# Differential attention by pairs of heads, with its scores, weighted sums and head norm placed between and inside projection slots

## What is computed

```
def diff_attention(xn, k_sh, v_sh, w_q, lam_params, subln_g, w_out, lambda_init):
    H, d = DIFF_HEADS, DIFF_HEAD_DIM                      # 8, 64
    q = (xn @ w_q).reshape(B, S, H, 2, d) * (d ** -0.5)
    lam = jnp.exp(jnp.sum(lp[0] * lp[1])) - jnp.exp(jnp.sum(lp[2] * lp[3])) + lambda_init
...
        s = jnp.einsum('bqhcd,bkhcd->bhcqk', qb, k_sh).astype(jnp.float32)
        s = jnp.where(kpos[None, :] <= qpos[:, None], s, -jnp.inf)
        p = jax.nn.softmax(s, axis=-1)
        a = p[:, :, 0] - lam * p[:, :, 1]
        return jnp.einsum('bhqk,bkhe->bqhe', a.astype(v_sh.dtype), v_sh)
...
    o = rms_norm(o, subln_g) * (1.0 - lambda_init)
    return o.reshape(B, S, H * 2 * d) @ w_out
```

## Time and profile before

| | us |
|---|---|
| median of 3 runs | 1465.35 |
| lowest, highest | 1465.29, 1469.29 |
| the profiled execution | 1465.31 |
| its span in the trace | 1463.5 |

### The profile page before, as it was taken

The page is one execution under the profiler, slowest core; times in us unless marked ns, Lnnn a source line. Parts: engine busy times, 40 slices in busy tenths (PEclk is TensorE's granted clock), DMA queues, the critical chain, the costliest instruction groups (busy, mean ns, idle before and its releaser), DMA issues.

```text
span 1463.5 us, 25191 instructions
## 1 busy us (share of the span) xinstructions
PE 1409.9 (96%) x9905; PEld 1301.1 (89%) x9905; DVE 914.7 (62%) x1162; ACT 697.6 (48%) x976; POOL 209.6 (14%) x142
## 2 busy tenths in 40 slices
PE   8999898998999999999999999999999997999998
PEld 8999888977998989988899997899987995899986
DVE  6875652046554577754584447688755677599964
ACT  5553355441222354433534455566654555566652
POOL 0000254302322000000000032022310000024410
PEclk9999999798999999999999999999999998999999
DMA  7444333120000445555455434455564440455553
GB/s 291 175 173 144 113 119 112 58 89 27 0 1 1 154 163 194 180 185 190 170 176 182 146 123 171 171 175 194 176 216 172 173 160 29 144 180 193 175 213 115
DMA packets 30315, 213.05 MB, mean 146 GB/s; under 512 B 3488, under 2 KB 3616, under 8 KB 5152
## 3 DMA queue, kind: packets, MB, share of 16 engines
q1 hardware_dynamic: 29088, 206.72, 40.1%
q0 software_dynamic: 1152, 5.24, 1.0%
HBM read 210.90 MB, written 1.05 MB: 145 GB/s over the span
## 4 chain that ended last, share of the span: by engine, by line
PE 87%; DVE 6%; ACT 4%; issue 2%; POOL 1%; DMA 1%; DVEq 0%; ACTq 0%; POOLq 0%; SPq 0%
PE lin L514 53%; PE lin L583 19%; PE aux L1991 2%; PE aux L2003 1%; PE aux L2001 1%; PE aux L1865 1%; PE aux L2072 1%; PE lin L620 1%; ACT whi L488 1%; POOL al L703 1%; PE aux L2084 1%; DVE wlo L495 1%; PE aux L1895 1%; DVE ht L1233 1%; DVE ro L1634 1%
## 5 line engine op out<-in xcount | busy, mean ns | idle before, releaser
L495 DVE TENSOR_TENSOR wlo<-raw,whi 128x2048 fp32r<-128x2048 f32 x176 | 409.5, 2331 | 190.4 <-ACT whi L488 190.1
L514 PE MATMUL lin<-xhi,whi 128*128 128x256 f32 (+1 forms) x1776 | 507.9, 286 | 1.8 <-DVE xlo L1244 1.8
L514 PE MATMUL lin<-xlo,whi 128*128 128x256 f32 (+1 forms) x1776 | 505.1, 284 | 0.0
L514 PE MATMUL lin<-xhi,wlo 128*128 128x256 f32 (+1 forms) x1776 | 502.7, 283 | 0.0
L488 ACT CAST whi<-raw 128x2048 fp32r<-128x2048 f32 x193 | 367.0, 1904 | 221.2 <-DMA raw<-in_stream 194.8
L514 PEld LDWEIGHTS lin<-xhi,whi 128*128 128x128 f32 x1776 | 334.9, 189 | 4.8 <-issue 4.0
L514 PEld LDWEIGHTS lin<-xhi,wlo 128*128 128x128 f32 x1776 | 337.1, 190 | 0.0
L514 PEld LDWEIGHTS lin<-xlo,whi 128*128 128x128 f32 x1776 | 335.7, 189 | 0.3
L681 POOL TENSOR_TENSOR wlo<-raw,whi 128x2048 fp32r<-128x2048 f32 x17 | 79.1, 4650 | 547.7 <-ACT whi L488 547.5
L1722 DVE SCALAR_TENSOR_TENSOR ft<-fy,par,ft 128x254 f32<-128x254 f32 (+1 forms) x176 | 90.9, 557 | 5.9 <-DVE ft L1722 0.2
L583 PE MATMUL lin<-whi,flo 128*128 128x512 f32 x176 | 69.8, 397 | 0.0
(11 more groups left out here) (378 smaller groups left out, 2295.2 us busy)
## 6 DMA issues: line engine op xcount, KB each, us to landing
raw<-in_stream SPq DMA_DIRECT2D x193, 1024.0 KB, 4.9
gp<-in_gains POOLq DMA_DIRECT2D x6, 512.0 KB, 3.9
c<-in_const SPq DMA_DIRECT2D x1, 1652.0 KB, 17.2
h<-in_x SPq DMA_DIRECT2D x2, 544.0 KB, 4.2
ht<-in_xtok POOLq DMA_DIRECT2D x1, 1024.0 KB, 6.8
c<-in_const POOLq DMA_DIRECT2D x1, 1024.0 KB, 5.0
out<-ht SPq DMA_DIRECT2D x1, 512.0 KB, 2.6
out<-ht SPq DMA_DIRECT2D x2, 256.0 KB, 2.2
```

The costliest lines, as they stand in the source:

```text
L495: nc.vector.tensor_tensor(wlo[:, s0 % 4], raw[:, s0 % 4], whi[:, s0 % 4].bitcast(F32), ALU.subtract).then_inc(lo_ready, 1)
L514: ins = nc.tensor.matmul(out, a, b, start=start and n == 0, stop=stop and n == 2)
```

## The change

- Keys and queries become one stream part `dkq` of 8 slots, in the order `DIFF`: keys 0, 1, 2, queries 0, 1, 2, keys 3, queries 3.
- Scores of pair n come as soon as both its slots are there: after slots 4, 5, 7 and after value slot 0.
- The weighted sums run by pairs of heads, each pair for both t (`HEAD_STEPS`), behind value slots 1, 2, 2 and 3.
- The head norm runs in two groups of four heads: group 0 around value slot 3 (its spread inside the slot), group 1 inside output slots 0 and 1. `keep_warm` around it is gone.
- The output slots change order: slot j belongs to half j % 2 and to heads of group j // 2, so slots 0 and 1 need heads 0-3 only.
- `dsq`, `dhi`, `dlo` move to memory that keys, queries and `x2` held.
- On ACT `x2hi` stands ahead of the conversions of slots 3 and 4; on DVE `x2lo` stands ahead of the eviction of slot 2. `lam` stands between them.

```diff
+DIFF = [("dk", 0), ("dk", 1), ("dk", 2), ("dq", 0), ("dq", 1), ("dq", 2), ("dk", 3), ("dq", 3)]
+HEAD_STEPS = [(t, 2 * n + q) for n in range(4) for t in range(2) for q in range(2)]
...
-        for t in range(2):
-            for hh in range(H1):
+        for n in range(4):
+            for t, hh in HEAD_STEPS[4 * n:4 * n + 4]:
                 use(hh % 2, f"dt{t}_{hh}")
                 if hh % 4 == 3:
-                    use(2 + hh // 4, f"dp{t}_{hh // 4}")
-        use(0, "ndsum")
-        for n in range(4):
-            use((n + 1) % 4, f"nd{n}")
+                    use(2 + t, f"dp{t}_{hh // 4}")
+            if n >= 2:
+                use(0, f"ndsum{n - 2}")
+                use(1, f"nd{2 * n - 4}")
+                use(0, f"nd{2 * n - 3}")
...
+            if name == "do":
+                return j % 2, j // 2
...
+            for b in range(4):
+                after(act, f"turn_diff{b}")
+            for kt in range(KT):
+                nc.scalar.activation(x2hi[:, kt], hf[:, kt // 2, kt % 2], ACT.Copy, scale=pcol("b_pre", kt))\
+                    .then_inc(S("x2hi"), 1)
...
+            def values(j):
...
+                ins.then_inc(pair_free[u % 2], 1)
+                load_hi(s + 3, 0)
...
+            for j in range(8):
+                load_hi(FIRST["dkq"] + j + 3, 0)
+                if j == 1:
+                    act.wait_ge(S("lam"), 1)
+                    nc.scalar.activation(lamt[:, 2:4], lamt[:, 0:2], ACT.Exp).then_inc(S("lam_exp"), 1)
+                if j >= 5:
+                    exponentials(j - 5)
+            values(0)
             exponentials(3)
...
+            values(1)
+            turned(0)
+            values(2)
+            turned(1)
+            heads_out(0)
+            turned(2)
+            heads_root(0)
+            values(3)
+            heads_high(0)
+            turned(3)
+            heads_out(1)
+            heads_root(1)
+            heads_high(1)
...
+            for k in range(2):
+                project(k)
...
+            for kt in range(KT):
+                dve.wait_ge(S("x2hi"), kt + 1)
+                ins = nc.vector.scalar_tensor_tensor(x2lo[:, kt], hf[:, kt // 2, kt % 2], pcol("b_pre", kt),
+                                                     x2hi[:, kt].bitcast(F32), ALU.mult, ALU.subtract)
+            ins.then_inc(S("x2lo"), 1)
+            project(2)
+            project(3)
...
+            project(4)
+            masked(0)
+            project(5)
+            masked(1)
+            project(6)
+            difference(0)
+            masked(2)
+            project(7)
+            difference(1)
+            load_lo(FIRST["dv"] + 3, 0)
+            masked(3)
+            difference(2)
+            load_lo(FIRST["dv"] + 4, 0)
+            difference(3)
+            load_lo(FIRST["dv"] + 5, 0)
+            heads_norm(0)
             load_lo(FIRST["dv"] + 6, 0)
-            dve_head_norm(dve, own, "nd", "subln")
+            heads_low(0)
+            heads_norm(1)
+            heads_low(1)
...
+            def project(k):
...
+                if k == 3:
+                    pe.wait_ge(S("x2lo"), 1)
...
+            project(0)
+            pe_spread("diff")
+            for k in range(1, 5):
+                project(k)
+            scores(0)
+            project(5)
+            scores(1)
+            project(6)
+            project(7)
+            scores(2)
+            values(0)
+            scores(3)
+            values(1)
+            weighted(0)
+            values(2)
+            weighted(1)
+            weighted(2)
+            heads_sum(0)
+            values(3, lambda: heads_spread(0))
+            weighted(3)
+            pe_post_layer(pe, "do", dhi, dlo, "ndlo", KT, lambda end: end // 2, between)
```

More of the change, by code:

```diff
@@ L586, in pe_post_layer @@
                         ins.then_inc(S("tile_" + tag), 1)
+                    if c == 0 and between:
+                        between(j)
                 ins.then_inc(slot_done, 1)
@@ L1116, in act_second @@
                 ins.then_inc(pair_free[u % 2], 1)
[L1117 to L1120, removed]
-            exponentials(3)
[L1122 to L1134, removed]
-                        g = hh // 4 - 1
-                        b = full(act, f"dp{t}_{g}")
-                        is_free(nc.scalar.copy(do[:, 4 * g:4 * g + 4, t * P:t * P + P], wide(b[:], P)), f"dp{t}_{g}")
-                        if t:
-                            act_head_squares(act, "nd", g)
-                if t == 0:
-                    load_hi(FIRST["dv"] + 6, 0)
@@ L1142, in act_second, with turned, heads_out @@
-            head_norm_act(act, "nd")
+                load_hi(s + 3, 0)
+            def turned(n):
+                for t, hh in HEAD_STEPS[4 * n:4 * n + 4]:
+                    W = P + t * P
+                    b = full(act, f"dt{t}_{hh}")
+                    k = HEAD_STEPS.index((t, hh))
+                    if k >= 2:
+                        weighted_sum_done(act, k - 2)
+                    is_free(nc.scalar.copy(aT[:, hh % 2, 0:1 + t], wide(b[:, 0:W], P)), f"dt{t}_{hh}")
+            def heads_out(g):
+                for t in range(2):
+                    b = full(act, f"dp{t}_{g}")
+                    is_free(nc.scalar.copy(do[:, 4 * g:4 * g + 4, t * P:t * P + P], wide(b[:], P)), f"dp{t}_{g}")
+                for t in range(2):
+                    after(act, f"dp{t}_{g}")
+                a = slice(4 * g, 4 * g + 4)
+                nc.scalar.activation(dsq[:, a], do[:, a], ACT.Square).then_inc(S("ndsq"), 1)
@@ new lines, in heads_root, with heads_high @@
+            def heads_root(g):
+                pair_done(act, pair_first["dkq"] + 7)
+                b = full(act, f"ndsum{g}")
+                if g:
+                    for n in (0, 1):
+                        full(act, f"nd{n}")
+                is_free(nc.scalar.activation(rhead[0:4, 0:SEQ], b[0:4, 0:SEQ], ACT.Sqrt, scale=1.0 / P,
+                                             bias=eps[0:4, 0:1]), f"ndsum{g}")
+            def heads_high(g):
+                for n in (2 * g, 2 * g + 1):
+                    after(act, f"nd{n}")
+                    a = slice(2 * n, 2 * n + 2)
+                    nc.scalar.copy(dhi[:, a], do[:, a]).then_inc(S("ndhi"), 1)
```

168 lines of the change are left out of this document (110 added, 58 removed).

## The result

| | before | after |
|---|---|---|
| median, us | 1465.32 | 1481.53 |
| lowest, highest | 1464.06, 1469.29 | 1480.06, 1484.19 |
| profiled execution | 1465.31 | 1481.37 |
| its span, mean granted clock | 1463.5, 0.974 | 1479.6, 0.968 |

The ratio is 1.0103, with a 95% interval of 1.009 to 1.0116. The prediction had the sign (slower, 0.81), but its 1474.5 stood for +9.2, and 16.2 was measured. The time lies outside the range of 1468 to 1479.

A forecast was written before the change was run, and what follows sets the result against it. PE was taken as the bound before, DVE as the bound of the stretch to the first sums. Layer +4.6, clock +3.4 and turn +1.2 made +9.2 on 1465.31, giving 1474.5 us; range 1468 to 1479.

The forecast's parts named there:

- sign (slower, 0.81): The whole kernel gets slower by more than 0.3% (4.4 us), chance 0.81.
- steps 1 to 5: Waits of PE: 3.7 us at `x2lo`, 7.3 at first sums, 5.3 at pairs 1 and 2, 7.0 last pair, none in output slots.
- 0.65 for rounding `dhi`: At the last pair, ACT rounds `dhi` before it copies, adding 0.65 us to a wait of 6.35.
- step 2: At pair 0's first product PE waits 7.3 us for `aT`, behind DVE's 37.9 us chain with queued conversions; bounds 5.5 and 9.5.
- The turn: At the passage to the next layer, DVE starts half 1 later: +1.2 us, bounds 0 and 2.3.
- The clock: Falls behind the waits of 7.3 and 6.4 us lose 1.7 us each: +3.4, bounds 0 and 5.
- nearer to 3.3 than to 4.43: `x2lo`'s 3.7 us wait was counted without clock loss: 3.3 us idle had kept full clock, 4.43 had halved it.
- rival A: `x2lo`'s wait before slot 3 drops the clock too: +2.1 us, 1476.6, chance 0.27.
- rival C: Short idle times at pairs 1 and 2 drop the clock: some 2 us more, 1476.5, chance 0.04.
- Rival B: At the long waits the clock costs nothing, as PE works little there: -3.4 us, 1471.1, chance 0.08.
- E: DVE's chain is some 3 us shorter and the last wait partly hidden: +0 to +4, 1465.3 to 1469.5, chance 0.09.
- D: Queued conversions don't delay `x2lo`, first sums and last pair: 14.0 us of waits and 3.4 of clock less, 1457.1, chance 0.10.

The follow-up runs named there:

- e1: The changed kernel with `x2lo` on DVE directly behind slot 0's eviction, ahead of the conversions of slots 3 and 4, and `lam` behind slot 1's eviction: 1476.15 us.
- e2: The changed kernel with output slot 14's conversions moved behind group 1's copies (ACT) and scaling (DVE), and group 0's rounding ahead of slot 11's eviction: 1475.78 us.
- e3: The changed kernel with value slot 10 and its eviction ahead of pair 0's sums and copies, slot 13's ACT conversion behind pair 1's copies: 1475.86 us.
- e4: The changed kernel with unused matmuls on ones in PE's three long waits (before slot 3, at pair 0, behind slot 11): 1475.97 us.
- e6: The changed kernel with only the spread of the head roots reading 128 partitions instead of 4: 1481.04 us.
- e10: e4 with the spread of the head roots reading 128 partitions instead of 4: 1473.34 us.
- e9: e7 with slot 13's conversion behind pair 2's copies on ACT and behind group 0's scaling on DVE: 1455.46 us.
- e5: The changed kernel with the edits of e1, e2 and e3 together: 1461.53 us, ratio 0.9962 to the kernel before.
- e7: e5 with the spread of the head roots reading 128 partitions instead of 4: 1456.90 us.
- e8: e7 with slot 13's conversion moved as in e9, and DVE's conversion of slot 17 moved behind the last residual: 1454.96 us.

## Why the prediction was off

**The waits (steps 1 to 5) were right.** By place, predicted and measured: slot 3 3.7 and 3.63; first products 7.3 and 6.81; pair 1 2.8 and 2.66; pair 2 1.9 and 1.76; last pair 7.0 and 6.33; output slots none and none. DVE's chain from the end of slot 4 (1164.36 less its semaphore) to the end of the fourth masking (1202.2) took 37.9 us, as walked through. What was too large was the 0.65 for rounding `dhi`: ACT's rounding from 1246.00 lies beside PE's transposes. Behind slot 3 the waits give 17.6 instead of 19.0, 1.4 less. PE's other work and short idle times take 99.3 us instead of 98.5 (97.9 and the four short waits of 0.15), 0.8 more. e1 (slot 3) and e2 (last pair) confirm their causes, since the wait went when the named conversions were taken from ahead of it, and so does e3 for pair 1. Pair 0's conversions were not moved in any run: e3 only filled the wait with a slot, and the first product came 78.7 us after the layer's start (1210.71 - 1132.02), where it had come after 77.9. That the conversions of slots 10 to 12 cost it what step 2 says was thus walked through but not tried.

**The turn** was predicted at +1.2. From the last output matmul to the next layer it took 4.60 us before and 6.03 after: +1.4.

**The clock is the step that failed.** It was entered as two falls of 1.7 us each, +3.4, "bounds 0 and 5". Measured are 10.5 us lost, 7.1 more than entered. The price itself was read low: 0.68 over the 7 us from 1211 is 4.5 us at half speed, not 4.2, and with the 0.57 us from 1210.43 on it is 5.0. With 0.2 for the start, -1.4, +0.8 and 0.2 at the turn the 7.1 come to 6.9, and 9.2 + 6.9 = 16.1, the distance of the profiled executions. That long waits drop the clock was right: with ones in the three of them, e4 kept it full there. Of the 7.1:

- The two counted falls cost 2.5 and 3.1 instead of 1.7 each: 2.2 more. The one at the last pair reached into the first output matmuls (from 1250.95 to about 1253), which are dense work.
- `x2lo`'s wait of 3.63 dropped the clock: 1.45. "nearer to 3.3 than to 4.43" was the wrong way to place it. This is rival A, given 0.27, with 2.1 as its price.
- Pairs 1 and 2: 1.7. This is rival C, given 0.04. Against it the prediction held that 2.31 us were passed at full clock. That was one case, and it went the other way in all six kernels with waits of 2.66 and 1.55 to 1.76 there. In four of the six (e1, e4, e6, e10) the clock fell 1.3 to 1.8 us after the wait of 2.66 ended, before the second idle time began, so the second isn't needed. PE's timeline and windows of e1:

```profile
1215.85 0.49 PE L2282 MATMUL aux<-aT,dv 128*128 128x128 f32 x2 [2.66 <-ACT aT L1135]
...
1220.91 0.80 PE L2282 MATMUL aux<-aT,dv 128*128 128x128 f32 x2 [1.55 <-ACT aT L1135]
```
```profile
1217.00:1219.00 2.00, 1.98 (x11) 1.94 (x10) 0.96 (x1) 0.89 (x3) 0.00 (x0) 0.56 0.14 57
```

- The fall behind the spread in slot 11: 1.7. No rival had it, though the trace of before shows one like it: the clock is 0.53 at 1238 to 1243, and at half from 1236 on, within and behind a spread over 8 partitions, with ones around it and no idle time of over 0.5 us (PE's timeline of before). The prediction read that fall as part of the old order's cost that goes away.

```profile
1233.25 4.62 PE L2084 MATMUL aux<-rstd,c 8*128 8x256 f32 x16 [0.42 <-DVE rstd L1568]
```

The mistake in method behind the two middle items is the same: a threshold was drawn through three idle times of one trace. That of 3.3 us, the lower bound, had a fall in e9 with the same work around it, so what passed once was no bound. A and C together, 1478.6 by the prediction, were each seen and each held improbable as if they depended on different facts; both follow once the threshold is in doubt. Rival C drew on the Trainium skill, "TensorE: Matmul & The Clock Gate", section "A second HAM failure mode: psum-queue depth-cycling", by which short idle times between groups of matmuls let the clock go down and up. The runs agree for pairs 1 and 2 (e3: a fall behind 1.90 us), though not each time: in e9 1.88 and 1.76 us passed at full clock.

**Rival B** fell with the 10.5 us lost, **E** with DVE's chain, which took its full 37.9 us, and the last wait of 6.33. **D** was wrong for this kernel, since the conversions do stand in the way. Its arithmetic was a fair guide to what the order could give: it had 14.0 us of waits from queued conversions, and e5, whose three moves go at the same waits, has 15.3 less. That the two are so close is partly luck, since in e5 a value slot fills most of pair 0's wait, which D did not have. This is where the expected gain of the change went.

**What stays open.** Why the same idle time or the same spread drops the clock in one kernel and not in another: 1.90 us did in e3, 1.87 to 1.89 at the same place in e5, e7, e8 and e9 did not; the 3.3 us at 360 us did in one of twelve profiles; 4 partitions in slot 11 did in five kernels and not in e1. The length of an idle time alone doesn't decide it. Whether a kernel has the same falls in each of its executions is open too, as each has one profile. Which of e6's other falls were longer by chance wasn't separated either.

## What to carry over

When independent work is moved between dense slots, walk through every queue that feeds it: here a weight conversion of 2 us, not urgent, stood ahead of an instruction that PE waited for, at four places, and moving them, with one value slot put ahead of one group of sums, turned +1.0% into -0.4% (e5); the spread over 128 partitions and slot 13's conversion brought -0.8% (e9). Count the clock for each place where PE waits or does small matmuls, not only for the longest wait (here falls stood behind waits of 1.90 to 3.63 us too), give it a range and not a threshold, and take the price of a fall from how much dense work follows it. Check a moved instruction against the next wait too: e3 and e8 each only handed part of the time on.

## What the runs showed of the hardware

- TensorE's clock fell within or behind idle times of 3.63 to 3.66 us in four of four kernels, of 3.14 in three of three, and of 2.66 with one of 1.55 to 1.76 some 4 to 5 us later in six of six; behind 1.88 and 1.76 in neither of two. Whether it falls isn't settled by the length: the same 3.3 us at 360 us passed in eleven profiles of twelve, and the same 2.2 to 2.5 us ahead of the layer in eight.
- The clock can fall to its lower level with PE busy all the time: in e2 PE was busy for 7.00 of 7.00 us at 1247 to 1254 and without a break after it, and the clock fell at 1256, behind eight matmuls that read 4 partitions. In five of six profiles it fell at the same matmuls in slot 11. The same with 128 partitions take as long (1.99 us for the eight) and had no fall in ten places.
- Matmuls on ones in three waits, where PE had nothing else to do, kept the clock there and cut the layer by 4.1 us; taking away the waits gave five times as much (21.7).
